# A hybrid decoder layer on one core: the decays' running sums made once, two heads' scores on the two row halves, one step for v, head weights and step sizes

## The reference, cut to what matters

```python
u = rms_norm(x); proj = u @ w_in      # z, xBC, dt, q, k, v, qi, ki, wi, gate_ssm, gate_att
# A: Mamba-2 mixer, 32 heads of 64, chunks of 128 tokens
dt = softplus(dt_raw + dt_bias); a = -exp(a_log)
a_cs = cumsum(dt * a) within a chunk                       # (chunk, token, head)
lmat = exp(where(causal, a_cs[t] - a_cs[s], -inf))         # per head
y_diag = (C B^T * lmat) @ (x * dt);  y_off from the first chunk's state
y = rms_norm((y_diag + y_off + d_skip * x) * silu(z))
# B: sparse attention. The indexer picks 64 keys of each query:
iscore = sum_h relu(qi_h . ki) * wi_h      # 8 heads of 64, one key head
s_h = q_h . k / 8 - slope_h * dist         # 16 heads of 64, one key/value head
p = softmax(s over the chosen causal keys); o_h = p @ v
x += (sigmoid(gate_ssm) * A + sigmoid(gate_att) * B) @ w_mix_out
x += cross_attention(...);  x += mixture of 32 experts, top 2;  out = rms_norm(x)
```

## Time and profile before

| | us |
|---|---|
| three runs, median (lowest to highest) | 1028.1 (1025.99 to 1028.37) |
| profiled execution | 1022.45 |
| its span, first to last instruction | 1020.7 |
| PE busy | 940.9 (92%) |
| weight loads (beside PE) | 666.5 |
| DVE, ACT, POOL busy | 447.0, 307.4, 108.8 |
| mean granted TensorE clock | 0.978 |

### The profile page before, as it was taken

How to read it: one execution, slowest core, us unless ns; L and a number is a source line. 1 busy time by engine, 2 the same in 40 slices (tenths; PEclk the granted TensorE clock), 3 DMA queues, 4 the chain that set the end, 5 groups by cost and what they waited for, 6 DMA issues and landing times.

```text
span 1020.7 us, 14481 instructions
## 1 busy us (share of the span) xinstructions
PE 940.9 (92%) x5791; PEld 666.5 (65%) x5791; DVE 447.0 (44%) x843; ACT 307.4 (30%) x505; POOL 108.8 (11%) x119
## 2 busy tenths in 40 slices
PE   3999899999999999989798999998989899898995
PEld 3999888898999999879675344444434353444443
DVE  4588996765766765464545121212111121211113
ACT  4455445657557434355333000000000000000002
POOL 1000016855452000000000000000000000000000
PEclk8999899999999999999999999999989999899999
DMA  9455353333325665468177999999999999999991
GB/s 219 140 165 166 127 163 124 125 124 107 102 87 174 196 190 180 165 234 289 54 254 293 423 421 422 420 422 422 422 422 422 422 422 422 422 422 422 422 412 43
DMA packets 110348, 277.72 MB, mean 272 GB/s; under 512 B 14866, under 2 KB 78402, under 8 KB 85722
## 3 DMA queue, kind: packets, MB, share of 16 engines
q1 hardware_dynamic: 110154, 276.51, 71.3%
q10 hardware_dynamic: 144, 0.52, 0.1%
HBM read 275.97 MB, written 1.05 MB: 271 GB/s over the span
## 4 chain that ended last, share of the span: by engine, by line
PE 62%; DMA 12%; DVE 12%; issue 6%; POOL 4%; ACT 4%; SPq 1%; DVEq 0%; POOLq 0%; ACTq 0%
PE bank L1851 18%; DMA up_b<-in_w_e_up_dram 12%; PE bank L1461 8%; PE bank L1463 8%; PE bank L1462 8%; PE bank L1881 8%; DVE lo_w L910 4%; PE bank L1821 3%; POOL work L566 3%; PE bank L1868 2%; ACT hi_w L592 2%; DVE work L1059 2%; DVE work L1060 1%; DVE xg L1395 1%; POOL ysT L554 1%
## 5 line engine op out<-in xcount | busy, mean ns | idle before, releaser
L1461 PE MATMUL bank<-u_hi,hi_w 128*128 128x256 f32 x624 | 185.0, 296 | 6.2 <-DVE lo_w L910 6.2
L1463 PE MATMUL bank<-u_hi,lo_w 128*128 128x256 f32 x624 | 178.8, 287 | 0.0
L910 DVE TENSOR_TENSOR lo_w<-raw_w,hi_w 128x2048 fp32r<-128x2048 f32 x68 | 154.7, 2280 | 54.8 <-ACT hi_w L592 54.6
L1462 PE MATMUL bank<-u_lo,hi_w 128*128 128x256 f32 x560 | 160.7, 287 | 0.0
L1851 PE MATMUL bank<-up_a,xg 128*64 128x512 f32 x256 | 123.8, 639 | 18.4 <-DMA up_b<-in_w_e_up_dram 18.4
L592 ACT ACTIVATE hi_w<-raw_w 128x2048 fp32r<-128x2048 f32 x68 | 128.3, 1889 | 32.4 <-PE bank L1463 29.1
L1461 PEld LDWEIGHTS bank<-u_hi,hi_w 128*128 128x128 f32 x624 | 122.2, 196 | 10.0 <-issue 8.7
L1851 PE MATMUL bank<-up_b,xg 128*64 128x512 f32 x256 | 123.9, 639 | 0.0
L1881 PE MATMUL bank<-down_a,moe_buf 128*64 128x512 f32 x256 | 113.2, 594 | 9.5 <-DVE xg L1395 7.6
L1463 PEld LDWEIGHTS bank<-u_hi,lo_w 128*128 128x128 f32 x624 | 121.9, 195 | 0.0
L869 ACT ACTIVATE y_pair_hi<-bank 128x512 fp32r<-128x512 f32 x32 | 17.4, 594 | 337.7 <-PE bank L1881 337.7
(11 more groups left out here) (323 smaller groups left out, 1761.0 us busy)
## 6 DMA issues: line engine op xcount, KB each, us to landing
raw_w<-in_w_in_dram SPq DMA_DIRECT2D x34, 1024.0 KB, 5.3
up_b<-in_w_e_up_dram SPq DMA_DIRECT2D x32, 1024.0 KB, 23.3
up_a<-in_w_e_up_dram SPq DMA_DIRECT2D x32, 1024.0 KB, 21.4
down_a<-in_w_e_down_dram SPq DMA_DIRECT2D x32, 1024.0 KB, 17.3
down_b<-in_w_e_down_dram SPq DMA_DIRECT2D x32, 1024.0 KB, 19.4
gate_a<-in_w_e_gate_dram SPq DMA_DIRECT2D x16, 1024.0 KB, 19.4
gate_b<-in_w_e_gate_dram SPq DMA_DIRECT2D x16, 1024.0 KB, 21.4
gate_c<-in_w_e_gate_dram SPq DMA_DIRECT2D x16, 1024.0 KB, 22.0
```

Of the source, the lines that this page charges most:

```text
L910: tt(lo_w[:, m % RING, 0:w], raw_w[:, m % RING, 0:w], hi_w[:, m % HI_RING, 0:w].bitcast(F32), ALU.subtract).then_inc(lo_done, 1)
L1461: mm(dst, left[0], right[0], start=first, stop=False)
L1462: mm(dst, left[0], right[1], start=False, stop=False)
L1463: return mm(dst, left[1], right[0], start=False, stop=last)
```

## The change

It has four parts.

1. `tm0` and `tm1` become one step `tm`, feature-major, 128 rows for 256 tokens, evacuated into `vwdT`. The load takes 24 more columns to fill the 128. PE turns it back with two transposes behind `fm_step("qi0")`, and DVE copies these into `small_tm` before it makes dt.
2. `k2` and `ki2` hold the key heads in both halves of the partitions, without zeros. `two_heads` makes four fp32 products of 64 rows, one head on the upper and one on the lower row half, a head's scores in one bank. The ReLU and the add of the position term follow the new layout.
3. The running sums of all 32 heads are made once as rows, four copies of the heads on 128 partitions: `dA_four` as fp32 weights times `tri`, two products behind xs3. ACT rounds them to fp32r in `acs_rows`; on partitions 32 to 63 DVE subtracts the high part, so that these hold the remainder. `cumsum_rows` is then one fp32r product of 256 columns a head, its weights a column of `head_sel` (ones at the head's high and low rows) repeated 128 times.
4. There is one step fewer, so the other steps change banks where these go by the step's number.

```diff
-SM_V, SM_WI, SM_DT, TM_W = 0, 64, 72, 104
+SM_V, SM_WI, SM_DT, TM_W = 0, 64, 72, 128
...
-        steps = (["k", "ki", "tm0", "tm1"] + [f"qi{b}" for b in range(4)] + [f"bc{b}" for b in range(8)]
+        steps = (["k", "ki", "tm"] + [f"qi{b}" for b in range(4)] + [f"bc{b}" for b in range(8)]
...
-                  [(SM_V, C_V, HEAD), (SM_WI, C_WI, IDX_HEADS), (SM_DT, C_DT, SSM_HEADS)]]
+                  [(SM_V, C_V, HEAD), (SM_WI, C_WI, IDX_HEADS), (SM_DT, C_DT, TM_W - SM_DT)]]
...
-            for d in (kz, kiz):
-                link(nc.gpsimd.memset(d[0:64, 1, :], 0.0))
-                link(nc.gpsimd.memset(d[64:128, 0, :], 0.0))
...
-            for name, d in (("k", kz), ("ki", kiz)):
-                n = STEP[name]
-                act.wait_ge(proj_ready, n + 1)
-                nc.scalar.activation(d[0:64, 0, :], bank[n % 2][0:64, 0:SEQ], ACT.Copy)
-                nc.scalar.activation(d[64:128, 1, :], bank[n % 2][64:128, 0:SEQ], ACT.Copy).then_inc(evac_act, 1)
-            for i in range(NT):
-                n = STEP[f"tm{i}"]
-                evac(f"tm{i}", small_tm[:, i, :], src=bank[n % 2][:, 0:TM_W])
+            for name, d in (("k", k2), ("ki", ki2), ("tm", vwdT)):
+                evac(name, d[:, :])
...
-                nc.scalar.activation(rel[:, b % 2, 0:256], bank[4][:, 0:256], ACT.Relu)
-                nc.scalar.activation(rel[:, b % 2, 256:768], bank[5][:, :], ACT.Relu).then_inc(idx_relu, 1)
+                nc.scalar.activation(rel[:, b % 2, 0:384], bank[4][:, 0:384], ACT.Relu)
+                nc.scalar.activation(rel[:, b % 2, 384:768], bank[5][:, 0:384], ACT.Relu).then_inc(idx_relu, 1)
...
+                if n == 14:
+                    act.wait_ge(acs_ready, 1)
+                    nc.scalar.activation(acs_rows[:, :], bank[6][:, 128:384], ACT.Copy).then_inc(acs_hi, 1)
...
+            tt(head_sel[0:64, :], ident[0:64, 0:32], ident[0:64, 32:64], ALU.add)
+            tt(head_sel[64:128, :], ident[64:128, 0:32], ident[64:128, 0:32], ALU.add)
             dve.wait_ge(prm_in, 16 * N_PRM)
...
-            wait_evac(dve, "tm1")
+            dve.wait_ge(vwd_turned, 1)
+            link(nc.vector.tensor_copy(small_tm[:, :, :], bank[2][:, 0:256].rearrange("p (i n) -> p i n", i=NT)))
...
+            dve.wait_ge(dt_ready, 1)
+            nc.vector.tensor_copy(dA_four[:, :, :, :], dA.unsqueeze(2).to_broadcast([P, NT, 4, SSM_HEADS]))\
+                .then_inc(dt_ready, 1)
...
+                dve.wait_ge(acs_hi, 1)
+                tt(acs_rows[32:64, :], bank[6][32:64, 128:384], acs_rows[32:64, :].bitcast(F32), ALU.subtract)\
+                    .then_inc(acs_done, 1)
...
-                    tt(pb[:, 0:128], bank[4][:, 128 * a:128 * a + 128], albi[:, a, 0:128], ALU.add)
-                    tt(pb[:, 128:384], bank[5][:, 256 * a:256 * a + 256], albi[:, a, 128:384], ALU.add)\
-                        .then_inc(sc_used, 1)
+                    tt(pb, bank[4 + a][:, 0:384], albi[:, a, :], ALU.add).then_inc(sc_used, 1)
...
-            w = use_unit("tm")
-            for i in range(NT):
-                b = bank_of(f"tm{i}")
-                for k in range(KT):
-                    last = product(b[:, 0:TM_W], [x[:, k, P * i:P * i + P] for x in u_parts],
-                                   [x[:, k, :] for x in w], k == 0, k == KT - 1)
-                last.then_inc(proj_ready, 1)
+            fm_step("tm", use_unit("tm"), 0, u_parts)
...
+            def two_heads(q, k, b):
+
+                for lo, hi in ((0, P), (P, SEQ)):
+                    for a in range(2):
+                        h = slice(64 * a, 64 * a + 64)
+                        last = mm(bank[4 + a][:, lo:lo + hi], q[h, b, lo:hi], k[h, 0:hi], start=True, stop=True)
+                return last
...
-                mm(bank[4][:, 0:256].rearrange("p (a s) -> p a s", a=2), qiT[:, b, 0:P], kiz[:, :, 0:P],
-                   start=True, stop=True)
-                mm(bank[5][:, :].rearrange("p (a s) -> p a s", a=2), qiT[:, b, P:SEQ], kiz[:, :, :],
-                   start=True, stop=True).then_inc(idx_ready, 1)
+                two_heads(qiT, ki2, b).then_inc(idx_ready, 1)
...
+                if b == 0:
+                    wait_evac(pe, "tm")
+                    for i in range(NT):
+                        last = tp(bank[2][:, P * i:P * i + P], vwdT[:, P * i:P * i + P], ident[:, :])
+                    last.then_inc(vwd_turned, 1)
...
-                    pe.wait_ge(dt_ready, 1)
+                    pe.wait_ge(dt_ready, 2)
+                    for i in range(NT):
+                        left = dA_four[:, i, :, :].rearrange("p a h -> p (a h)")
+                        last = mm(bank[6][:, P + P * i:2 * P + P * i], left, tri[:, :], start=True, stop=True)
+                    last.then_inc(acs_ready, 1)
...
-                    for i in range(NT):
-                        left = dA[:, i, 2 * b + a:2 * b + a + 1].to_broadcast([P, P])
-                        last = mm(bank[4 + b % 2][:, 256 * a + P * i:256 * a + P * i + P], left, tri[:, :],
-                                  start=True, stop=True)
+                    left = head_sel[:, 2 * b + a:2 * b + a + 1].to_broadcast([P, P])
+                    last = mm(bank[4 + b % 2][:, 256 * a:256 * a + 256], left, acs_rows[:, :], start=True, stop=True)
```

More of the change, by code:

```diff
@@ L115, in hybrid_block @@
         qiT = place("qiT", [P, 4, SEQ], "misc")
-        kz = place("kz", [P, 2, SEQ], "misc", skip=4 * KB)
-        kiz = place("kiz", [P, 2, SEQ], "misc", skip=6 * KB)
+        k2 = place("k2", [P, SEQ], "misc", skip=4 * KB)
+        ki2 = place("ki2", [P, SEQ], "misc", skip=5 * KB)
+        acs_rows = place("acs_rows", [P, SEQ], "misc", F32R, skip=6 * KB)
+        vwdT = place("vwdT", [P, SEQ], "misc", skip=7 * KB)
+        dA_four = place("dA_four", [P, NT, 4, SSM_HEADS], "misc", skip=7 * KB)
         isc, selm, dist, caus = (place(n, [P, 384], "misc", skip=8 * KB + 1536 * i)
@@ L177, in hybrid_block @@
         sel2 = sb("sel2", [2, P])
+        head_sel = sb("head_sel", [P, SSM_HEADS], F32R)
         drow = sb("drow", [2, 16])
@@ L233, in hybrid_block @@
         cb_ready, cb_done = sem("cb_ready"), sem("cb_done")
-        acs_ready, acs_done = sem("acs_ready"), sem("acs_done")
+        acs_ready, acs_hi, acs_done = sem("acs_ready"), sem("acs_hi"), sem("acs_done")
+        vwd_turned = sem("vwd_turned")
         xt_ready, xdt_done = sem("xt_ready"), sem("xdt_done")
@@ L300, in rows @@
             return w[0, 512 * half:512 * half + 512, c0:c0 + 512].rearrange("(t p) n -> p t n", p=P)
-        units, LAST_STEP = [("kk", None, KT), ("tm", None, KT)], {"kk": "ki", "tm": "tm1"}
+        units, LAST_STEP = [("kk", None, KT), ("tm", None, KT)], {"kk": "ki", "tm": "tm"}
         for kind, w, c0, n in (("qi", w_in, C_QI, 2), ("bc", w_in, C_B, 4), ("xs", w_in, C_XS, 8), ("q", w_in, C_Q, 4),
@@ L341, in hybrid_block @@
                       for j in range(8) if f"{k}{j}" in UN}
-        FIRST_STEP.update({"k": "kk", "tm0": "tm"})
+        FIRST_STEP.update({"k": "kk", "tm": "tm"})
         FIRST_STEP.update({f"so{j}": f"so{j}" for j in range(8)})
@@ L1011, in _ @@
                         w = hi - lo
-                        src = rel[:, b % 2, 128 * a:128 * a + 128] if i == 0 else \
-                            rel[:, b % 2, 256 + 256 * a:512 + 256 * a]
+                        src = rel[:, b % 2, 384 * a + lo:384 * a + hi]
                         wi = small_tm[:, i, SM_WI - SM_V + h:SM_WI - SM_V + h + 1]
@@ L1567, in _ @@
                 if b == 3:
-                    pe.wait_ge(dt_ready, 1)
+                    pe.wait_ge(dt_ready, 2)
                     mm(bank[6][:, 0:32], tri[:, :], dA[:, 0, :], start=True, stop=True)
                     mm(bank[6][:, 32:64], tri[:, :], dA[:, 1, :], start=True, stop=True)
-                    mm(bank[6][:, 64:96], ones[:, :], dA[:, 0, :], start=True, stop=True).then_inc(acs_ready, 1)
+                    mm(bank[6][:, 64:96], ones[:, :], dA[:, 0, :], start=True, stop=True)
+                    for i in range(NT):
+                        left = dA_four[:, i, :, :].rearrange("p a h -> p (a h)")
+                        last = mm(bank[6][:, P + P * i:2 * P + P * i], left, tri[:, :], start=True, stop=True)
+                    last.then_inc(acs_ready, 1)
                 if b in (5, 9):
@@ L1604, in scores @@
                     pe.wait_ge(sc_used, 2 * b)
-                mm(bank[4][:, 0:256].rearrange("p (a s) -> p a s", a=2), qT[:, b, 0:P], kz[:, :, 0:P],
-                   start=True, stop=True)
-                mm(bank[5][:, :].rearrange("p (a s) -> p a s", a=2), qT[:, b, P:SEQ], kz[:, :, :],
-                   start=True, stop=True).then_inc(sc_ready, 1)
+                two_heads(qT, k2, b).then_inc(sc_ready, 1)
             def prob_transposes(b):
@@ L1632, in values @@
                 if b == 0:
-                    pe.wait_ge(acs_done, 2)
+                    pe.wait_ge(acs_done, 3)
                 for a in range(2):
```

## The result

| kernel | median us (lowest to highest, runs) | profiled execution | its span | ratio to before, 95% interval |
|---|---|---|---|---|
| before | 1027.95 (1025.99 to 1028.37, 4) | 1022.45 | 1020.7 | |
| after | 1018.15 (1016.68 to 1018.71, 4) | 1018.71 | 1017.0 | 0.9913 (0.9895 to 0.993) |

The changed kernel is 9.8 us faster, 0.9%. The forecast was 1021.3, in a range of 1015.0 to 1027.3. Later 27 runs of before gave a median of 1026.05 (1022.34 to 1028.81); against that one the gain is 7.9 us. So the size of the gain is known to about two microseconds, its sign is not in doubt.

A forecast was written before the change was run, and what follows sets the result against it. PE bounds the g stage, PE and DVE alternate in the convolution, DMA bounds the experts. +0.9 - 1.35 + 2.3 + 0.36 - 2.8 - 6.25 = -6.85: 1015.6 profiled, 1021.3 from the runs' median; range 1015 to 1027.3.

The forecast's parts named there:

- DVE late, +0.9: Start-up: DVE starts the step sizes later, at 35.4, so the low half of qi1 and qi2 come 0.9 us later.
- Clock, +2.3: Around qi2: with PE nearly idle some 5 us, the granted clock falls and 2.3 us are lost after 43.7.
- Three indexers, -1.35: Indexer groups on PE's path: each takes 0.85 us on row halves, saving 0.45, three times.
- the z stage, -2.8: Scores: -0.55 survives at scores(0), and the other five groups save 0.45 each, 2.25.
- `decay_biases`, +0.36: Convolution, bounded by DVE: DVE's added subtraction of 32 x 256 elements costs 0.36 us.
- g stage, -6.25: Decays: -0.6 for cumsum(0) to (4), -7.15 for eleven others, 1.5 given back to a chain of other engines.
- Experts unchanged: Last 471.9 us, DMA-bound: the stage keeps its length and a shift at 548 us passes on in full.
- rival A: Clock does not fall and the g stage keeps its 1.5: -10.7, 1017.4; chance 0.17.
- B: Row halves do not overlap: 1.44 instead of 0.85 in nine groups, change -1.5, 1026.6; chance 0.10.
- E: Row halves hide no weight load: 2.8 us a group, change +10.7, 1038.8; chance 0.04.
- D: Within a half, loads cannot run beside that half's own product: 1.08 a group, change -4.8, 1023.3; chance 0.06.
- C: g stage: POOL, DVE and ACT hold the 5.20 period, 5.65 of its saving gone: -1.2, 1026.9; chance 0.08.

The follow-up runs named there:

- e6: After, with DVE making the low half of unit qi1 before it waits for the turned rows ahead of the step sizes; 1012.19 us, ratio 0.9877.
- e7: After, with the two transposes of `vwdT` moved ahead of qi0; 1015.93 us, ratio 0.991.
- e1: Before, unchanged, run and traced once more; 1024.53 us, ratio 1.0008, profiled execution 1028.03.
- e5: After, unchanged, run once more beside eight new runs of before; 1018.05 us, ratio 0.9928.
- e8: After, with DVE doing y_out ahead of the next unit's low half in the g stage; 1016.95 us, ratio 0.9922.
- e12: After, with every group of scores in the z stage made twice; a single run, 1021.8 us, used for its trace alone.
- e2: Before plus only the row halves for indexer and scores (part 2); 1022.9 us, ratio 0.9973.
- e3: Before plus only the decays' running sums (part 3); 1019.92 us, ratio 0.9947.
- e4: Before plus only v, head weights and step sizes as rows (part 1); 1027.4 us, ratio 1.0015.
- e9: After with the edits of e6 and e8 together; 1012.08 us, ratio 0.9857.
- e10: After with the edits of e6, e7 and e8 together; 1011.18 us, ratio 0.9861.
- e11: e9 with `tm0` and `tm1` token-major as in before, so without part 1; 1014.35 us, ratio 0.9888.

## Why the prediction was right, step by step

- **DVE late, +0.9.** The mechanism is right: step sizes at 35.37 (35.4 forecast), qi2 at 43.66 (43.7), idle 4.24 us, and e6 and e7 show that it was the place of the low half behind the step sizes and nothing on PE. That the size fits so well is luck. The second execution of before (e1) has its step sizes at 35.73 and qi2 at 43.68, as late as after; four traces of this start-up (after, e5, e8, e12) have qi2 from 43.51 to 44.03, on average 0.6 behind the two of before. What does not scatter is the part of `dA_four`: from the step sizes to the low half 5.94 us instead of 5.61.
- **Clock, +2.3.** Right in kind. PE worked 3.7 us at 0.50. This does not cost half, as the prediction reckons: the timeline of PE of after has the products 0.213 us apart there and 0.12 at full clock, which is 44% lost.

```profile
44.47 0.41 PE L1466 MATMUL bank<-u_hi,hi_w 128*128 128x256 f32 x1
44.68 0.41 PE L1467 MATMUL bank<-u_lo,hi_w 128*128 128x256 f32 x1
...
47.55 0.28 PE L1466 MATMUL bank<-u_hi,hi_w 128*128 128x256 f32 x1
47.66 0.28 PE L1467 MATMUL bank<-u_lo,hi_w 128*128 128x256 f32 x1
```

  From qi2 to the next step after takes 5.54 us, e6 3.91: 1.6 lost, and 2.2 in e5, 2.1 in e8, 1.7 in e12. e6 takes the idle time away, and the fall with it.
- **Three indexers, -1.35, and the z stage, -2.8.** The mechanism was right, the price of a group 0.85 was right (0.86), but what it saves was mis-sized: 0.45 was the difference of two groups, and the cost of switching lies partly outside of them. This is the period of the z stage in before, from the timeline of PE:

```profile
187.84 0.60 PE L1605 MATMUL bank<-kz,qT 128*128 128x256 f32 x2
...
196.52 0.60 PE L1605 MATMUL bank<-kz,qT 128*128 128x256 f32 x2
```

  8.68, against 8.40 after: 0.28 saved a group. The arithmetic alone would save 1.29 - 0.65 = 0.64; so 0.36 goes into changing to the row halves and back, of which 0.21 lies inside of the 0.86 and 0.15 around it. PE is busy all through both periods, so the difference is its own. Three indexers then save some 0.85 (e2: 0.9). The z stage went from 88.83 to 86.57, -2.3 instead of -2.8.
- **`decay_biases`, +0.36.** The way from the sums to `xdt` grew by 0.6 in both after and e3, and not in e2 and e4. The subtraction takes 0.45 from its start to the next instruction's, and the one ahead of it, which before took 0.11, takes 0.22, together 0.56: this term was mis-sized.
- **g stage, -6.25.** Measured 84.26 - 90.83 = -6.57, and 84.28 in e3 where it is alone. Its terms: a free period 5.20 to 4.54, -0.66 (0.65), eleven times; up to y(3) -0.7 instead of -0.6; against it 0.43 at y(7), 0.43 at y(11) and 0.48 at y(15), 1.3 together (1.5). The stalls come before every fourth y, not 0.25 in every second period as the sum had it, and e8 shows their cause. One reading was wrong without harm: of the four waits in the earlier trace rows three lie in the stage's start, the fourth (0.26) before y(15).
- **Experts unchanged.** From gather to last down product 463.2 us before, 465.0 after, 464.8 in e1 and 463.3 in e5: no effect of the change.
- **Sum.** The terms as after and before have them are +0.9 - 0.9 + 1.6 + 0.6 - 2.3 - 6.6 = -6.7 against a forecast of -6.85: what the row halves did not save (1.0) is nearly made up by the clock (0.7) and the g stage (0.3), so the sum is better than its terms. At the last `sum_squares` two executions of after stand 5.7 to 7.5 us ahead of two of before, 6.6 on average; the medians have -6.6, -7.9 or -9.8, as one takes the 8, 27 or 4 runs of before. The first comparison's 1018.15 lies below the forecast's own band (1019 to 1023.6) and next to the 1017.4 of rival A, whose mechanism did not come; it is in the range all the same. The forecast made its sum against the profiled execution and put it on the median of three, though the two lay 5.65 apart. e1 is 5.6 longer than that execution, 0.9 in the start-up and the rest behind 322 us, where its clock falls in places where that of before does not; with these the change has nothing to do.

**Rivals.** A does not hold (the clock fell, the stalls are there), though e9 and e10 build it, and more: what was counted as given back is got back by two edits. B (halves one after the other) and E (no load hidden) are out by 0.86 and 0.65 a group, D by 0.65. C is out by the period of 4.54; what it said of the chain is true for one period in four.

## What to carry to other kernels

Time that is taken from an engine arrives at the end only where the others are ready for it: part 1 made PE 2.4 us quicker and ran it into a wait on DVE that took all of this, and behind the wait the low clock cost another 1.6. One low half issued ahead of the wait gave back 5.9 us, more than twice what the part saves on PE. An experiment that takes a part out again has to be read for what else goes with it: e11 also brought back a stretch of low clock. When a product changes shape, measure the period around it and not the group: what is paid for the change of mode stands ahead of and behind it. And put a sum on a median only after one knows what the profiled execution had that the runs had not.

## What the runs showed of the hardware

- Two fp32 products of 64 rows on the two row halves, 128 and 256 columns, run side by side: 0.65 us a group when it repeats (e12). Going into this form and back costs 0.36 us a time (8.68 - 8.40 against 1.29 - 0.65). The Trainium skill (TensorEngine Tiling (Array Packing), Key Properties) says "Mode switching requires drain"; the 0.36 us fit that, but no run here shows what PE does in them.
- An fp32r product with one weight column repeated 128 times costs what any other of 256 columns does: the period fell by 0.66, where 0.24 against 0.89 us gives 0.65.
- At the 1.2 GHz level fp32r products of 256 columns start 0.213 us apart, at 2.4 GHz 0.12 (after, 44.5 to 47.7): such a stretch costs 44% of its length.
- The clock also falls with PE busy: for 3.4 us from between 33.5 and 35.7 in each of the five traces with the 104-column products, in none of the nine without. What of that step brings it was not tested.
- The same kernel, with the same wait of PE ahead of it (2.36 us), had the granted clock fall at 441.9 in one execution and not in another; places like this one, at 427 to 445 and at 526 to 557 us, are in some executions of before, after and the variants, and not in others. The cause was not looked into.
